# A two-layer decoder trunk on one core: when VectorE does taps and norms, and where the norm of o and its gate stand

## The reference

```python
p = h @ w_in
qkv = silu(causal_short_conv(qkv, conv_w))           # four taps
q = l2norm(q) * 128 ** -0.5;  k = l2norm(k)          # 8 heads of q and k, 16 of v
g = -exp(a_log) * softplus(a + dt_bias); beta = sigmoid(bb)
o = gated_delta_chunked(q, k, v, g, beta)            # chunks of 64, state of 16 heads
o = rms_head(o, norm_g) * silu(z)
return o @ w_out
```

```python
sc, pos = top_k(cand, 16); gate = softmax(sc)        # routing: 8 heads x 16 experts a token
ue = take(u, ib); act = gb * gelu(einsum('nd,nkd->nk', tb, ue))   # dots
ve = take(v, ib); y = einsum('nk,nkd->nd', act, ve)
```

## Time and profile before

| | us |
|---|---|
| median of 3 runs | 2079.04 |
| lowest, highest | 2062.32, 2084.35 |
| profiled execution, device time | 2087.26 |
| its span, first to last instruction | 2085.4 |
| TensorE busy | 1543.9 (74%) |
| VectorE busy | 1162.0 (56%) |
| GpSimd busy | 1082.1 (52%) |
| ScalarE busy | 387.0 (19%) |
| moved by DMA | 703.83 MB, mean 338 GB/s |

### The profile page before, as it was taken

The page is one execution under the profiler, slowest core; times in us unless marked ns, Lnnn a source line. Parts: engine busy times, 40 slices in busy tenths (PEclk is TensorE's granted clock), DMA queues, the critical chain, the costliest instruction groups (busy, mean ns, idle before and its releaser), DMA issues.

```text
span 2085.4 us, 21695 instructions
## 1 busy us (share of the span) xinstructions
PE 1543.9 (74%) x8116; PEld 1015.8 (49%) x8116; DVE 1162.0 (56%) x2739; ACT 387.0 (19%) x900; POOL 1082.1 (52%) x1031
## 2 busy tenths in 40 slices
PE   7997976978796668868788766886888651656556
PEld 6743872546453656656566464674766420000001
DVE  5454385655632878577344296858733348746430
ACT  1212100000001631431211253153221010000000
POOL 0000167667655465655554546565565265666664
PEclk8998966555557779879988887988999885776778
DMA  9453599999999988897999998798799988999997
GB/s 348 181 198 141 202 390 389 410 411 411 411 403 351 372 333 286 338 347 251 392 381 411 334 352 339 256 395 327 238 405 414 363 301 309 374 367 382 349 359 277
DMA packets 173111, 703.83 MB, mean 338 GB/s; under 512 B 23360, under 2 KB 23744, under 8 KB 155728
## 3 DMA queue, kind: packets, MB, share of 16 engines
q0 software_dynamic: 147456, 536.94, 68.2%
q1 hardware_dynamic: 25552, 165.53, 19.9%
HBM read 701.34 MB, written 1.05 MB: 337 GB/s over the span
## 4 chain that ended last, share of the span: by engine, by line
PE 27%; issue 18%; DVE 15%; POOL 11%; DMA 9%; another core or an unknown queue 6%; ACT 4%; SPq 0%; POOLq 0%; ACTq 0%; DVEq 0%
PE PS L1595 8%; DVE ub L1126 6%; POOL ub L1949 5%; DMA ub<-in_peer_u,idx 5%; POOL vb L1960 4%; PE PS L1701 3%; PE PS L1654 3%; PE PS L1637 2%; DMA ring<-in_gdn_z 2%; PE PS L1915 1%; POOL mods L1960 1%; ACT ring L1420 1%; PE PS L1885 1%; PE PS L1866 1%
## 5 line engine op out<-in xcount | busy, mean ns | idle before, releaser
L1949 POOL DMA_INDIRECT ub<-in_peer_u,idx x512 | 551.2, 1077 | 447.2 <-DVE dots L1126 282.4
L1126 DVE CUSTOM_DVE_ANT_0 ub<-ub,h 128x1024 f32<-128x1024 f32 x384 | 462.0, 1222 | 208.3 <-DMA ub<-in_peer_u,idx 141.6
L1960 POOL DMA_INDIRECT vb<-in_peer_v,idx x337 | 354.8, 1053 | 191.0 <-issue 94.7
L1595 PE MATMUL PS<-vb,z 128*32 128x512 f32 x1348 | 382.1, 782 | 92.6 <-DMA vb<-in_peer_v,idx 57.6
L1126 DVE CUSTOM_DVE_ANT_0 ub<-ub,PS 128x1024 f32<-128x1024 f32 x128 | 154.5, 1220 | 102.2 <-DMA ub<-in_peer_u,idx 73.7
L1595 PEld LDWEIGHTS PS<-vb,z 128*32 128x32 f32 x1348 | 63.5, 128 | 303.6 <-issue 170.7
L1654 PEld LDWEIGHTS PS<-c_act,ring 128*128 128x128 f32 x896 | 171.1, 295 | 46.6 <-issue 46.5
L1654 PE MATMUL PS<-c_act,ring 128*128 128x1 f32 x896 | 172.0, 324 | 13.1 <-issue 13.0
L1595 PE MATMUL PS<-mods,z 128*32 128x512 f32 x444 | 139.2, 817 | 44.4 <-DMA mods<-in_peer_v,idx 24.9
L1960 POOL DMA_INDIRECT mods<-in_peer_v,idx x111 | 114.8, 1034 | 33.8 <-issue 33.8
L1701 PE MATMUL PS<-hT,ring 128*128 128x128 f32 x1024 | 125.2, 282 | 9.5 <-DMA ring<-in_gdn_qkv 5.4
(11 more groups left out here) (322 smaller groups left out, 2281.3 us busy)
## 6 DMA issues: line engine op xcount, KB each, us to landing
ring<-in_gdn_qkv SPq DMA_DIRECT2D x32, 1024.0 KB
ring<-in_ada_late SPq DMA_DIRECT2D x28, 1024.0 KB
ring<-in_peer_wq SPq DMA_DIRECT2D x24, 1024.0 KB
ring<-in_ada_w SPq DMA_DIRECT2D x10, 2048.0 KB, 8.2
ring<-in_gdn_z SPq DMA_DIRECT2D x16, 1024.0 KB
ring<-in_gdn_w_out SPq DMA_DIRECT2D x16, 1024.0 KB
ring<-in_gla_w_in SPq DMA_DIRECT2D x6, 2048.0 KB, 8.0
ub<-in_peer_u,idx POOLq DMA_INDIRECT x512
```

Source lines behind the costliest of these rows:

```text
L1126: dve.tensor_tensor_reduce(out=ub[:, n % UB, :], in0=ub[:, n % UB, :], in1=by_token, scale=1.0, scalar=0.0, op0=ALU.mult, op1=ALU.add, acc ...
L1595: last = pe.matmul(y[32 * j:32 * j + 32, e, :], z[:, j, 28 * b:28 * b + 32], rows[:, e * 512:(e + 1) * 512], start=False, stop=False, skip ...
L1949: pool.indirect_dma_start(ub[:, n % UB, :], None, u_rows, off).then_inc(u_land[n % UB].sem, 16)
L1960: pool.indirect_dma_start(rows, None, v_rows, off).then_inc(land.sem, 16)
```

## The change

No computation is added or taken away. It moves steps within the queues:

- The taps of VectorE are due 4 units later (first part) and 6 later (second part, with a due time of its own); gc 2 later; the reciprocal of the q/k norm, its spreading and its two products 2.5 later, their sums and roots 2 later; silu 0.5 later.
- At the start of a core, TensorE waits only for the q/k norm. The waits for the last staged group and the last silu move from the decay rows to the transposes of v.
- The squares of o are taken at the end of each core (8 heads each) instead of behind each z silu, the root directly behind the second eight, and VectorE's reciprocal and product at `at0` + 321 instead of + 351.
- z blocks are due every 5 units instead of 4. Silu, gate, four transposes and copy of a pair of z blocks are due at + 10, + 12.5, + 14 and + 15 of each ten units, between the z blocks, instead of all together behind them.
- Output product due from + 362, every 4.5, instead of from + 358, every 5; norm 4 and queries and scores 3 units later.

On ScalarE the following order changes with it: the copy of `z` in the last phase (due at W + 444.6) now stands ahead of the copy of the third group of queries (W + 447 instead of W + 444).

```diff
@@ VectorE
-                                    yield p0 + 15 * un + 12
+                                    yield p0 + 15 * un + 16
...
                                     dve.tensor_tensor(out_, tapped_by[:, 0], tapped_by[:, 1], ALU.add)
+                                    yield p0 + 15 * un + 18
                                     dve.wait_ge(tapped.sem, nth(tapped, 8, kk, 2 * un + 1))
...
-                                        yield p0 + 39
+                                        yield p0 + 41.5
                                         dve.wait_ge(l2_root.sem, l2_root.at(kk + 1))
                                         dve.reciprocal(inv8[:], inv8[:]).then_inc(inv_made.sem, 1)
                                         for e in range(2):
-                                            yield p0 + 41 + e
+                                            yield p0 + 43.5 + e
                                             normalised(e)
...
-                            yield at0 + 351
+                            yield at0 + 321
                             dve.wait_ge(o_root.sem, o_root.at(t + 1))
                             link(dve.reciprocal(rs16[:], rs16[:]))
...
                             for b in range(4):
-                                yield at0 + 352 + b
+                                yield at0 + 316 + 10 * b + 12.5
                                 dve.wait_ge(z_out.sem, nth(z_out, 4, t, b))
...
-                                yield at0 + 376 + 20 * e
+                                yield at0 + 382 + 18 * e
@@ ScalarE
+                                def o_squares(hf):
+                                    for v_ in range(hf * HH, (hf + 1) * HH):
+                                        last = act.activation(junk[:, v_ * P:(v_ + 1) * P], o_of(t)[:, v_, :], ACT.Square, accum_out=ss16[:, v_:v_ + 1])
+                                    return last
+
+                                if hf == 0:
+                                    yield core.at("U", 0) + core.dt * 11
+                                    act.wait_ge(o_out.sem, nth(o_out, 4, t, 1))
+                                    o_squares(0)
+                            act.wait_ge(o_out.sem, nth(o_out, 4, t, 3))
+                            link(o_squares(1))
+                            act.activation(rs16[:], ss16[:], ACT.Sqrt, bias=eps[:], scale=1.0 / P).then_inc(o_root.sem, 1)
...
                             for b in range(4):
-                                yield at0 + 316 + 8 * b + 4
+                                yield at0 + 316 + 10 * b + 10
                                 act.wait_ge(g_used.sem, index["z", t, 2 * b + 1] + 1)
                                 act.activation(zbuf[:, b * 512:(b + 1) * 512], PS[:, 3 + b, :], ACT.Silu).then_inc(z_out.sem, 1)
...
+                                yield at0 + 316 + 10 * b + 15
+                                turned_o(b)
@@ TensorE
                                 yield core.at("GR", 0)
-                                pe.wait_ge(stage_in.sem, nth(stage_in, 4, kk, 3))
                                 pe.wait_ge(qk_ready.sem, nth(qk_ready, 2, kk, 1))
-                                pe.wait_ge(conv_silu.sem, nth(conv_silu, 4, kk, 3))
                                 decay_rows(0)
...
                                     ps = into(("VN", gq))
+                                    if gq == 0:
+                                        pe.wait_ge(stage_in.sem, nth(stage_in, 4, kk, 3))
+                                        pe.wait_ge(conv_silu.sem, nth(conv_silu, 4, kk, 3))
...
                             for b in range(8):
-                                yield at0 + 316 + 4 * b
+                                yield at0 + 316 + 5 * b
...
                                 last.then_inc(g_used.sem, 1)
-                            for b in range(4):
-                                yield at0 + 352.5 + b
...
+                                if b % 2 == 0 and b:
+                                    yield at0 + 316 + 5 * b + 4
+                                    turn_o(b // 2 - 1)
+                            yield at0 + 360
+                            turn_o(3)
...
-                                    yield at0 + 358 + 10 * e + 5 * part
+                                    yield at0 + 362 + 9 * e + 4.5 * part
...
-                                    yield at0 + 412 + 10 * un + 4 * bb
+                                    yield at0 + 415 + 10 * un + 4 * bb
```

More of the change, by code:

```diff
@@ new lines, in mixer, with turned_o @@
+                            act.wait_ge(o_out.sem, nth(o_out, 4, t, 3))
+                            link(o_squares(1))
+                            act.activation(rs16[:], ss16[:], ACT.Sqrt, bias=eps[:], scale=1.0 / P).then_inc(o_root.sem, 1)
+                            def turned_o(b):
+                                act.wait_ge(o_turned.sem, nth(o_turned, 4, t, b))
+                                act.activation(oT[:, 4 * b:4 * b + 4, :], PS[:, 3 + (b + 4) % 5, :].rearrange("p (v n) -> p v n", n=P), ACT.Copy, scale=gng[:]).then_inc(oT_made.sem, 1)
@@ L1501, in mixer @@
-                                for e in range(4):
-                                    v_ = 4 * b + e
-                                    last = act.activation(junk[:, v_ * P:(v_ + 1) * P], o_of(t)[:, v_, :], ACT.Square, accum_out=ss16[:, v_:v_ + 1])
-                            link(last)
-                            act.activation(rs16[:], ss16[:], ACT.Sqrt, bias=eps[:], scale=1.0 / P).then_inc(o_root.sem, 1)
-                            for b in range(4):
-                                yield at0 + 353 + b
-                                act.wait_ge(o_turned.sem, nth(o_turned, 4, t, b))
-                                act.activation(oT[:, 4 * b:4 * b + 4, :], PS[:, 3 + (b + 4) % 5, :].rearrange("p (v n) -> p v n", n=P), ACT.Copy, scale=gng[:]).then_inc(oT_made.sem, 1)
@@ L1510, in mixer @@
-                            yield at0 + 361
+                                yield at0 + 316 + 10 * b + 15
+                                turned_o(b)
+                            yield at0 + 363
                             gate_rows(2 * t + 2, t)
-                            yield at0 + 397
+                            yield at0 + 401
                             act.wait_ge(x_new.sem, nth(x_new, 2, t, 1))
                             squares(2 * t + 1, t)
-                            yield at0 + 400
+                            yield at0 + 404.0
@@ L1516, in mixer @@
                             normed(2 * t + 1, t)
-                            yield at0 + 404
+                            yield at0 + 408.0
                             modulated(2 * t + 1, 4)
-                            yield at0 + 408
+                            yield at0 + 412
                             for e in range(2):
@@ L1532, in mixer @@
                                 if un:
-                                    yield at0 + 412 + 10 * un + 9
+                                    yield at0 + 415 + 10 * un + 9
                                     scores1_out(un - 1)
-                            yield at0 + 455
+                            yield at0 + 458
                             scores1_out(3)
@@ L1710, in mixer @@
                                     if un == 2:
-                                        yield p0 + 37
+                                        yield p0 + 39
                                         sums()
-                                        yield p0 + 40
+                                        yield p0 + 42.5
                                         for e in range(2):
@@ L1857, in mixer, with turn_o @@
                                         last.then_inc(ds_done.sem, 1)
+                            def turn_o(b):
+                                pe.wait_ge(gated.sem, nth(gated, 4, t, b))
+                                if b:
+                                    pe.wait_ge(z_out.sem, nth(z_out, 4, t, b - 1))
+                                for e in range(4):
+                                    last = pe.transpose(PS[:, 3 + (b + 4) % 5, e * P:(e + 1) * P], o_of(t)[:, 4 * b + e, :], ident[:])
+                                last.then_inc(o_turned.sem, 1)
                             for b in range(8):
-                                yield at0 + 316 + 4 * b
+                                yield at0 + 316 + 5 * b
                                 if b == 0:
@@ L1867, in mixer @@
                                 last.then_inc(g_used.sem, 1)
-                            for b in range(4):
-                                yield at0 + 352.5 + b
-                                pe.wait_ge(gated.sem, nth(gated, 4, t, b))
-                                if b:
-                                    pe.wait_ge(z_out.sem, nth(z_out, 4, t, b - 1))
-                                for e in range(4):
-                                    last = pe.transpose(PS[:, 3 + (b + 4) % 5, e * P:(e + 1) * P], o_of(t)[:, 4 * b + e, :], ident[:])
```

(7 more changed lines are left out.)

16 lines of the change are left out of this document (7 added, 9 removed).

## The result

| | before | after |
|---|---|---|
| median, us | 2075.85 (4 runs) | 2055.76 (4 runs) |
| lowest, highest | 2062.32, 2084.35 | 2051.36, 2062.11 |
| ratio | | 0.9898, 95% interval 0.9861 to 0.9936 |
| span of the profiled execution | 2085.4 | 2056.0 |

The change makes the kernel 1.0% faster, about 21 us by the ratio and 20 by the medians, where I had forecast 12 and called "within 1%" the likeliest outcome. The two profiled executions lie 29.4 us apart, more than the medians: the one of before was 11 us above its median of 2075.85, the one of after 2.

A forecast was written before the change was run, and what follows sets the result against it. It took the mixer's chain (TensorE, ScalarE, VectorE by turns) to pace the core and DMA bytes from the gate on. Terms -2.9 - 6.0 - 1.0 - 2.0 = -11.9 us took the median 2079.0 to 2067 us, range 2046 to 2090.

The forecast's parts named there:

- within 1%: Whole kernel: a time within about 1% (20.8 us) of before, which measurement can't tell from no change; chance 0.64.
- sign of being right: Mixer windows of the second layer: they would take 503 to 513 us, one of several such signs.
- Taps and norms: VectorE's taps and q/k norms behind more dots: -2.9 us, between -5.3 and +4.3, with gelu's wait of 1.33 us gone.
- +4.3 bound: First halves: taps held up by two dots with routing steps, 9.6 us lost in all, against 5.3 gained.
- Decay rows: Start of core: ScalarE's 2.23 us wait ahead of the exponentials goes in four halves; two thirds of 8.9, -6.0 us.
- Norm of o: Last z silu to output product: chain from 15.4 to 7.1 us, yet only -1.0 us in all, bounds 0 and -14.0.
- a full DMA hides it: From the gate on: DMA at 0.95 to 1.02 leaves 1.0 us of room in the first window, none in the second.
- The tail: Window tails: later query products let V sets go ahead of score groups, -2.0 us, bounds 0 and -4.2.
- All hidden: Core stage: its gains are given back once DMA is full, only the tail's 2 us stay: 2077 us; chance 0.28.
- The tail hole closes: Second window's tail: z copy ahead of query copy ends a 13.93 us TensorE wait: 2053 us; chance 0.20.
- Gates behind rows: Around z: gates wait for dots whose rows land late, holding TensorE's transposes, 20.0 us lost per window: 2102 us; chance 0.12.
- sign of being wrong: Gate transposes: TensorE waits over 8 us in a window at its four transposes, one of several such signs.

The follow-up runs named there:

- e1: Kernel before with only the taps and q/k norms (with their sums, roots and spreads) due later; 2074.15 us, ratio 0.9992.
- e10: Kernel before with four copies of 0.52 us on ScalarE between decay rows and first exponentials of each quarter; third chip, 2009.94 us, ratio 1.0047.
- e11: Kernel before with squares, root and reciprocal of o early, gates, transposes and copies still behind the last z block; third chip, 2001.21 us, ratio 1.0002.
- e12: Kernel before with 12 copies of 0.52 us on ScalarE ahead of the root of o; third chip, 1999.62 us, ratio 1.0001.
- e3: Kernel before with only the norm of o, gate and transposes moved, and later due times up to the queries; 2062.73 us, ratio 0.9932.
- e5: The whole change without its edit to the taps and q/k norms; second chip, 2051.11 us, ratio 0.9893 to before.
- e7: Kernel before with the norm-of-o edit and half the bytes of the z, out and wq1 loads; second chip, 2034.12 us, ratio 0.9812.
- e2: Kernel before with only the waits for last staged group and last silu moved to the transposes of v; 2063.49 us, ratio 0.9927.
- e4: Kernel before with only the query products and scores due 3 units later; 2070.25 us, ratio 0.9979.
- e6: Kernel before with half the bytes of the z, out and wq1 loads; second chip, 2038.36 us, ratio 0.9828.
- e8: Kernel before with 100 one-column copies on ScalarE put in ahead of everything; second chip, 2068.12 us (one execution).

## Why the prediction came out as it did

The range (2046 to 2090) held the time; the forecast itself, 12 us less, was too small, and the gain is 21. The two windows, 497.6 and 501.0 us in the profile, are shorter than the 503 to 513 that I had given as a sign of being right. By its steps:

**Taps and norms, forecast -2.9.** Measured alone -1.7, with an interval of 5 us either way, and nothing that can be seen on top of the other parts. The gelu's wait did vanish, as said. In e1's profile the first halves are shorter, 2.1 and 1.6 us to the first k product, and the second halves longer, 3.6 and 2.9 us from taps to k product (59.2 and 57.9 us against 55.6 and 55.0). That is the kind of give-back that the +4.3 bound stood for, in other halves than I had placed it. Kernels that leave the second halves alone have 47 to 56 us there, so two single profiles don't size it. The term agrees with the measurement, which can't tell it from nothing.

**Decay rows, forecast -6.0.** Measured -15.2, from -20.6 to -9.6. The term was mis-sized. I counted one wait of 2.2 us in each half, 8.9 in all. In the first halves the second group moved up too, by 6.0 and 4.7 us against before's profile, and the chain became 11.5 to 14.8 us shorter. I also let VectorE take back a third of it, because it is idle for a quarter of the core. That it takes back anything is not shown (e10: 9.4 us for 8.9 inserted), and that it takes back a third is not excluded (5.8 at the low end): VectorE's idle time there is in large part time in which it waits for this same chain.

**Norm of o, forecast -1.0 with -14 as its bound.** Measured -14.1 on the chip of the first set, from -19.3 to -8.9. The length of the chain was right: 9.5 us with a V set of 2.5 in it, where I had 7.1. So was "a full DMA hides it", where DMA is full: e11 and e12 show it on the third chip, with 6.8 and 22 us of chain and one time. The term that was mis-sized is what I built on it, 1.0 us for both windows because DMA is nearly full at z. The traces don't show how it became 14. The gates between the z blocks cost time ahead of the last silu: from the last state to that silu the first window has 42.9 to 43.4 us in after, e3, e5 and e7, which have the edit, and 35.4 to 36.3 in e1, e2, e4 and e6, which don't (before's 43.7 and e8's 42.2 stand apart). From the last state to the output product it is 52.1 to 52.6 us with the edit and 50.7 to 59.1 without it; in the second window 56.2 to 61.1 and 59.1 to 63.5. So the edit mostly moved time within this stretch, and the rest of its gain lies elsewhere. In e3's profile the second window's tail keeps the stall, and the earlier stages differ by as much as between kernels that don't touch them. With lighter loads, on another chip, the edit was worth 4 us. The 14.1 is measured, its way is open.

**The tail, forecast -2.0.** Measured -4.4, from -9.3 to +0.6, at the edge of the bounds of 0 and -4.2 that I gave it, and not told from nothing.

**The rivals.** "All hidden" fell with e2 and e10: the core gives its time to the kernel. "The tail hole closes" named the right place and the wrong cause, and the releaser that I called unknown is TensorE. The stage with the hole did shrink in after, 80.0 to 70.3 us in the second window; but e4 has the z copy ahead of the query copy and keeps the hole (78.8 us). Had I let the hole go by itself, the forecast would have been 2053, near the 2056 measured. "Gates behind rows" was seen in its beginning: VectorE's gates wait 16.4 and 10.7 us, and TensorE waits 8.3 and 9.1 at the transposes, above the 8 us that I had set as a sign of being wrong. The stage ahead of the last silu is 7.6 us longer in the second window, and in the first some 7 us longer than in e1, e2, e4 and e6. So the price was some 7 us in a window and not 20, a little more than the 6 that the shorter chain won.

**The sum.** The terms as measured alone give -35.4, the whole is -21. Two terms were too small by 9 and 13 us, and the parts together brought less than apart. That the range held is in part luck: 35.4 us less would have been below its low end. Why they bring less together is not shown. One reading is that they fill the same idle transfer time (DMA at 0.94 and 0.92 instead of 0.92 and 0.89 over the windows), but the bytes are the same, so this share rises with any shorter window. On the third chip two of the parts bring 6.4 us; my terms for these two, -6.0 and -1.0, would have been near it there, with the norm of o at nothing in e11, which has half of that edit.

## What to carry to other kernels

Time on a chain by turns of engines was paid here in full or nearly so where DMA had a share of 0.80 to 0.88, though VectorE was idle for a fifth to a quarter of the time: that idle time is in large part the chain itself. Fifteen microseconds of chain were free where DMA stood at 1.02. So cut the trace by stage and ask for each how full the transfers are. And gains of edits measured alone must not be added without a run of them together.

A second lesson is on measuring: the same kernel took 2076.8 and 1999.9 us on two chips, and two edits worth 0.7% each on the one were worth 0.3% together on the other. Parts that are to be compared belong on one chip. And one profile before and one after don't size a stage: e8, with the mixer of before, had windows of 500.0 and 510.2 us where before's profile has 513.1 and 518.4.

## What was unexpected of the hardware

- One program, two chips: 2076.8 and 1999.9 us, with near equal busy times of VectorE and GpSimd and the granted clock at 0.80 and 0.82 over the span. On the first two chips, in ten tails of a window, a signal of TensorE reached ScalarE 12.5 to 15.3 us after the record of the work had ended, with no transfer of instructions in between; on the third all 596 came within 0.06 us. The traces of the first two also lack more than a third of all signals, so "no releaser" in a profile can mean that a record is missing.
- Loads of 1024 KB and rows gathered by index share DMA at 408 to 413 GB/s for 110 us and more, at a share of 1.02; shorter stretches of 48 to 55 us reached 414.
- Silu, root and exponentials each want another table set: every load took 1.28 us (71 in before, 73 in after). After the change the root of the next norm pays one more of them, as forecast:
```profile
1077.09 1.28 ACT L1343 ACT_TABLE_LOAD   x1
1078.38 0.30 ACT L1343 ACTIVATE nrs<-nss,eps 128x1 f32<-128x1 f32 x1
```
The Trainium skill (ScalarE: Activation LUTs, What ACT_TABLE_LOAD costs) gives about 1.28 us for the load and 2.66 with a drain. The trace agrees on the load and has no room for the drain behind it: from the load's end to the start of the root it is 0.01 us.
